# Token halves across the borders of dense stages in a two-layer streaming encoder kernel

## The reference

```
x += 0.5 * post(SwiGLU_1(pre(x)))
h  = pre(x); P = h @ w_in            # attention, recurrence and convolution inputs
x += post(concat(A, B, C) @ w_out)
x += 0.5 * post(SwiGLU_2(pre(x)))

def rms_norm(x, g):
    return x * rsqrt(mean(x * x, axis=-1) + EPS) * g
```

## Time and profile before

| | |
|---|---|
| time, median of 3 runs (lowest to highest) | 3127.04 us (3125.63 to 3131.36) |
| the profiled execution's own time | 3130.29 us |
| its span | 3128.5 us |
| PE busy | 2851.9 us, 91% |
| DVE busy | 1490.7 us, 48% |
| ACT busy | 943.2 us, 30% |
| POOL busy | 476.5 us, 15% |
| mean granted TensorE clock | 0.944 of full |
| PE idle before the lead's products, on DVE's low part (L390) | 55.1 us over 28 waits |
| DMA share of 16 engines' span, main queue | 19.5% |

### The profile page before, as it was taken

The page is one execution under the profiler, slowest core; times in us unless marked ns, Lnnn a source line. Parts: engine busy times, 40 slices in busy tenths (PEclk is TensorE's granted clock), DMA queues, the critical chain, the costliest instruction groups (busy, mean ns, idle before and its releaser), DMA issues. The chain is left out here.

```text
span 3128.5 us, 43457 instructions
## 1 busy us (share of the span) xinstructions
PE 2851.9 (91%) x18052; PEld 2667.2 (85%) x18052; DVE 1490.7 (48%) x1863; ACT 943.2 (30%) x1240; POOL 476.5 (15%) x325
## 2 busy tenths in 40 slices
PE   8999997996778899999989999979957787999997
PEld 7999997895546799999989999968945477999997
DVE  5333336477764453333363324365776635442333
ACT  4221223245134233122332212233452333321222
POOL 2000002047230300000120000120671313000001
PEclk9999998998789899999999999989976898999998
DMA  4222212112011021221212121222121011212111
GB/s 153 71 71 85 69 59 77 63 68 65 16 61 54 28 95 61 74 81 65 83 54 77 61 91 62 72 71 81 35 65 76 1 68 39 84 57 91 67 61 67
DMA packets 51694, 209.59 MB, mean 67 GB/s; under 512 B 14048, under 2 KB 14432, under 8 KB 35712
## 3 DMA queue, kind: packets, MB, share of 16 engines
q1 hardware_dynamic: 50544, 205.36, 19.5%
q10 hardware_dynamic: 1040, 2.69, 0.2%
HBM read 197.85 MB, written 10.19 MB: 66 GB/s over the span
## 5 line engine op out<-in xcount | busy, mean ns | idle before, releaser
L274 PE MATMUL ps<-hr,wr 128*128 128x320 f32 x11424 | 1728.0, 313 | 90.8 <-DVE hr L390 55.1
L274 PEld LDWEIGHTS ps<-hr,wr 128*128 128x128 f32 x11424 | 1698.5, 190 | 113.2 <-issue 55.2
L274 PE MATMUL ps<-hid,wr 128*128 128x320 f32 x4224 | 620.8, 309 | 0.0
L274 PEld LDWEIGHTS ps<-hid,wr 128*128 128x128 f32 x4224 | 619.9, 188 | 0.0
L269 DVE TENSOR_TENSOR wr<-stage,wr 128x2048 fp32r<-128x2048 f32 x164 | 377.2, 2300 | 221.9 <-ACT wr L265 221.9
L265 ACT ACTIVATE wr<-stage 128x2048 fp32r<-128x2048 f32 x164 | 312.2, 1903 | 340.7 <-DVE arena L579 267.2
L562 DVE TENSOR_TENSOR arena<-ps,arena 128x640 f32<-128x640 f32 x88 | 72.5, 824 | 546.7 <-PE ps L274 545.1
L536 POOL TENSOR_TENSOR arena<-arena 128x640 f32<-128x640 f32 x28 | 44.3, 1583 | 1736.9 <-ACT arena L514 1736.9
L505 ACT ACTIVATE arena<-arena 128x640 f32<-128x640 f32 x88 | 65.1, 740 | 803.0 <-DVE arena L562 803.0
L728 POOL TENSOR_TENSOR proj<-proj,arena 128x640 f32<-128x640 f32 x120 | 206.5, 1721 | 102.7 <-ACT arena L720 88.8
L1183 PE MATMUL ps<-proj 128*128 128x256 f32 x264 | 87.4, 505 | 69.8 <-issue 44.8
(11 more groups left out here) (208 smaller groups left out, 2191.3 us busy)
## 6 DMA issues: line engine op xcount, KB each, us to landing
stage<-in_wgu SPq DMA_DIRECT2D x88, 1024.0 KB, 4.8
stage<-in_wd SPq DMA_DIRECT2D x32, 768.0 KB, 4.2
stage<-in_w_in SPq DMA_DIRECT2D x24, 1024.0 KB, 4.9
stage<-in_wd SPq DMA_DIRECT2D x32, 640.0 KB, 3.9
stage<-in_w_out SPq DMA_DIRECT2D x8, 1024.0 KB, 5.2
arena<-in_ic SPq DMA_DIRECT2D x16, 256.0 KB, 2.7
hf<-bias_table SPq DMA_DIRECT2D x2, 2048.0 KB, 10.4
arena<-in_kc SPq DMA_DIRECT2D x16, 256.0 KB, 5.9
```

The costliest lines, as they stand in the source:

```text
L274: mm = pe.matmul(out, w(s), v(t), start=start and n == 0, stop=stop and n == 2)
```

## The change

A border is passed by the tokens in two halves of 320, and the stages from the output projection of one layer to the projection of the next stand in one program block.

- The last tile before a border computes half 0 in full, then half 1. Between the products of half 1 PE sums half 0's squares and broadcasts its factor. DVE evicts the two halves apart. The last square (`direct=1`), or the last two after an output projection (`direct=2`), go from ACT to PE without POOL. In a feed-forward stage ACT now makes the next weights' high part ahead of the square of the last tile but one.
- The lead makes y, x, high, low and square in pieces of 320 columns: all channel blocks of half 0, then all of half 1. The factor is copied by ACT from PSUM to `rs` in SBUF, from where DVE reads it. Half 1's eviction, square, root and factor stand between the pieces of half 0, and so does the split of the second weight tile. POOL adds seven times for a half, without clearing `ssum`.
- PE takes two weight tiles for each channel block, and fills all eight banks: tile 0 for blocks 0 to 3 of half 0, tile 1 for the same, both for the rest; at the end blocks 6 and 7 of half 1, tile 0 first and then tile 1.
- The sums over channels of `x` squared go to columns 320 to 479 of banks in use; the sums for `y` and the factor go to banks 1 and 3.
- In the projection the first four column blocks fill eight banks. `weigh_in` moves to block 4, the logits follow in groups of three from the end of block 4 to the middle of block 8, the streams follow half a block later than before.
- `par` is loaded after the second FFN's last weights. The result is stored in 16 pieces.

The core of the diff:

```diff
+            def pe_total(self, pe, a, row, last=False):
+                src = ssum if row is None else sqb[:, row]
                 for t in range(5):
+                    mm = pe.matmul(ps[0:64, 1, 5 * a + t:5 * a + t + 1],
+                                   src[:, a * HALF + 64 * t:a * HALF + 64 * t + 64], ones[:, 0:1],
+                                   start=row is None and t == 0, stop=last and t == 4, skip_group_check=True)
...
+            def pe_products(self, pe, tile_done):
+                self.tile_done = tile_done
+                self.pe_wait_weights(pe, 0)
+                for k in range(4):
+                    pe.wait_ge(self.split, self.of_k(0, k))
+                    self.pe_part(pe, 0, k, 0)
+                    if k == 2:
+                        self.pe_middle(pe, 1)
+                self.pe_wait_weights(pe, 1)
+                for k in range(4):
+                    self.pe_part(pe, 1, k, 0)
+                self.pe_factor(pe, 1)
+                for k in range(4, KD):
+                    pe.wait_ge(self.split, self.of_k(0, k))
+                    for j in range(2):
+                        self.pe_part(pe, j, k, 0)
+                self.pe_wait_copied(pe)
+                for k in range(KD - 2):
+                    pe.wait_ge(self.split, self.of_k(1, k))
+                    for j in range(2):
+                        self.pe_part(pe, j, k, 1)
+                    if k == 1:
+                        self.pe_x_total(pe, 0)
+                    if k == KD - 3:
+                        self.pe_x_total(pe, 1)
+                pe.wait_ge(self.split, self.of_k(1, KD - 1))
+                for j in range(2):
+                    for k in range(KD - 2, KD):
+                        self.pe_part(pe, j, k, 1)
...
             def act_part(self, act):
+                self.act_y(act)
                 for k in range(KD):
+                    self.act_x(act, 0, k)
+                    if k == 1:
+                        self.act_y_square(act, 1)
+                        split_hi(act, 0, 1, self.n0)
+                    if k == 3:
+                        self.act_y_root(act, 1)
+                    if k == 5:
+                        self.act_y_copy(act, 1)
+                for k in range(KD):
+                    self.act_x(act, 1, k)
+                    if k == 2:
+                        self.act_root(act, 0)
+                self.act_root(act, 1)
...
+            def dve_y(self, dve, a, k):
+                dve.scalar_tensor_tensor(out=y[:, k, half(a)], in0=y[:, k, half(a)],
+                                         scalar=par[:, self.post + k:self.post + k + 1], in1=rs[:, half(a)], op0=ALU.mult,
...
+            def dve_part(self, dve, evict):
+                dve.wait_ge(par_in, 16 * (self.m // 3) + 16)
+                evict(0)
+                self.dve_y_rsqrt(dve, 0)
+                for a in range(2):
+                    dve.wait_ge(self.y_copied, self.of_y(a))
+                    self.dve_y(dve, a, 0)
+                    for s in range(KD + 1):
+                        if s < KD:
+                            self.dve_x(dve, a, s)
+                        if s < KD - 1:
+                            self.dve_y(dve, a, s + 1)
+                        if s >= 1:
+                            self.dve_split(dve, a, s - 1)
+                        if a == 0 and s == 2:
+                            evict(1)
+                        if a == 0 and s == 3:
+                            split_lo(dve, 0, 1, self.n0)
+                        if a == 0 and s == 5:
+                            self.dve_y_rsqrt(dve, 1)
+                for a in range(2):
+                    self.dve_rsqrt(dve, a)
...
+                down_tile(KD // 2 - 1, 0)
...
+                last_part(0, range(KB_F)).then_inc(last_half, 1)
+                pe.wait_ge(y_summed, S + KD + 1)
+                pe.wait_ge(evac, dn + KD + 1)
+                nxt.pe_total(pe, 0, None)
+                last_part(1, range(3))
+                nxt.pe_total_direct(pe, 0)
+                last_part(1, range(3, 5))
+                nxt.pe_factor(pe, 0)
+                last_part(1, range(5, KB_F)).then_inc(used, 1)
...
+                if ahead:
+                    act.wait_ge(used, dn + KD - 1)
+                    split_hi(act, KD // 2 - 1, 0, dn + 2)
+                act.wait_ge(evac, dn + KD + 1)
+                act.wait_ge(y_summed, S + KD - 1)
+                act.activation(sqb[:, 0], y[:, KD - 2], ACT.Square).then_inc(y_squared, 1)
...
+                last_part(0, range(KD)).then_inc(last_half, 1)
+                pe.wait_ge(summed, KD - 1)
+                pe.wait_ge(evac, OUTP + 5)
+                nxt.pe_total(pe, 0, None)
+                last_part(1, range(2))
+                nxt.pe_total_direct(pe, 0)
+                last_part(1, range(2, 3))
+                nxt.pe_factor(pe, 0)
+                last_part(1, range(3, KD)).then_inc(used, 1)
...
+        def BANK_OF(q):
+            return 2 * q if q < 4 else 2 * (q % 2)
+        SELECT_FROM, LOGIT_STEPS, TAPS_FROM, TAPS_EACH = 4, 8, 11, 3
...
+                def beside(q, second):
+                    u = 2 * (q - SELECT_FROM) + second
+                    if u == 0:
+                        weigh_in()
+                    elif u < LOGIT_STEPS + 1:
+                        for n in LOGITS_AT[u - 1]:
+                            logit(n)
...
+                lead.pe_products(pe, block_done)
+                for q in range(4, NB):
+                    n, c, _ = BLOCKS[q]
+                    if c == 0:
+                        pe.wait_ge(w_lo, PROJ + n + 1)
+                    pe.wait_ge(p_evac, {4: 1, 5: 2}.get(q, q - 1))
```

More of the change, by code:

```diff
@@ L15 @@
+from collections import namedtuple
 from contextlib import ExitStack
@@ L294, in pair_of_tiles, with half, __init__ @@
             mm.then_inc(used, 1)
[L296 to L301, removed]
+        def half(a):
+            return slice(a * HALF, (a + 1) * HALF)
         class Lead:
-            def __init__(self, m, n0, factor, post, pre):
+            def __init__(self, m, n0, factor, post, pre, direct=1):
@@ L328, in pe_start, with pe_middle, pe_x_total @@
                 mm.then_inc(self.y_factor, 1)
[L330 to L336, removed]
+            def pe_middle(self, pe, a):
+                self.pe_total(pe, a, None)
+                self.pe_total_direct(pe, a)
+            def pe_x_total(self, pe, a):
+                pe.wait_ge(self.summed, self.sums(a) + KD - 1)
+                for c in range(2):
+                    mm = pe.matmul(ps[:, 4 * a + 2 * c, HALF:HALF + 160], ones[:], ssum[:, half(a)][:, 160 * c:160 * c + 160],
+                                   start=True, stop=True)
+                mm.then_inc(self.total, 1)
@@ new lines, in pe_part, with pe_wait_weights @@
+            def pe_part(self, pe, j, k, a):
+                for c in range(2):
+                    at_ = k * 256 + 128 * c
+                    mm = three(pe, ps[:, 4 * j + 2 * c + a, 0:HALF], lambda s: wr[:, j, s, at_:at_ + 128],
+                               lambda t: hr[:, t, k, half(a)], k == 0, k == KD - 1)
+                    if a and k == KD - 1:
+                        self.tile_done(mm, j, c)
+            def pe_wait_weights(self, pe, j):
+                pe.wait_ge(w_lo, self.n0 + j + 1)
+                pe.wait_ge(evac, self.n0 + j + 1)
@@ new lines, in dve_rsqrt @@
+            def dve_rsqrt(self, dve, a):
+                dve.wait_ge(self.root, 2 * self.m + a + 1)
+                dve.reciprocal(rs[:, half(a)], rs[:, half(a)]).then_inc(self.rsqrt, 1)
+            def dve_part(self, dve, evict):
[18 more added lines that the diff above has]
+                            self.dve_y_rsqrt(dve, 1)
+                for a in range(2):
+                    self.dve_rsqrt(dve, a)
+                dve.wait_ge(self.rsqrt, 2 * self.m + 2)
@@ new lines, in evict_last @@
+            def evict_last(dve, a):
+                if a:
+                    dve.wait_ge(used, chunks[1][3] + KD)
+                else:
+                    dve.wait_ge(last_half, f + 1)
+                dve.tensor_tensor(y[:, KD - 1, half(a)], y[:, KD - 1, half(a)], ps[:, 4 + a, 0:HALF],
+                                  ALU.add).then_inc(nxt.y_evicted, 1)
+                if a:
+                    dve.sem_inc(evac, 1)
+            return Stage(sync, tensor, scalar, gpsimd, vector), evict_last
@@ new lines, in evict_last @@
+            def evict_last(dve, a):
+                if a:
+                    dve.wait_ge(used, OUTP + 4)
+                else:
+                    dve.wait_ge(last_half, 1)
+                for c in range(2):
+                    cp = dve.tensor_copy(y[:, KD - 2 + c, half(a)], ps[:, 4 + 2 * c + a, 0:HALF])
+                cp.then_inc(nxt.y_evicted, 1)
+                if a:
+                    dve.sem_inc(evac, 1)
+            return Stage(sync, tensor, scalar, gpsimd, vector), evict_last
@@ L789, in build, with project_and_select @@
```

(2 more changed lines are left out.)

1143 lines of the change are left out of this document (598 added, 545 removed).

## The result

The changed kernel takes 3148.66 us (median of 4 runs, 3145.86 to 3150.56), the kernel before 3128.53 us beside it. The ratio on record is 1.0058, with an interval of 1.0046 to 1.0070 (the two medians alone would give 1.0064): slower, by 0.58%. The forecast had 3129. The time lies inside the wide range (3100 to 3150), at its edge, and outside the likeliest case's own (3118 to 3140).

A forecast was written before the change was run, and what follows sets the result against it. The prediction took PE, busy 91% of the span, plus its holes as the bound. Gains of 6.1, 3.9 and 1.7 us less losses of 2.8 and 11.1 gave -2.2: 3127.0 + 2.2 = 3129 us, range 3100 to 3150.

The forecast's parts named there:

- the likeliest case: Whole kernel: the sum as worked out, 3129 us, with its own range of 3118 to 3140; chance 0.48.
- The opening: Kernel start: tile 2 in effect at 72.9 us against 61.8, where there was no hole; 11.1 us lost.
- The holes behind the two tiles: Before tile 2: nothing covers eviction to weights, so PE stands 7.1 us after an FFN; in the projection tile 2 starts at 59.25.
- POOL's add held by the weight split: Last tile before an FFN border: DVE's low part holds up POOL's add, so PE waits 1.4 us.
- The clock's term for the sparse work: Lead, 13.85 to 20.6 us: a second clock fall slows block 2, sums and block 3; 2.5 us, bounds 0 and 3.5.
- Half 0: Lead behind an FFN: DVE begins half 0's y at 12.2 us and half 1 at 32.75.
- Half 1: Lead behind an FFN: DVE starts at 32.75 us, last low part at 48.4, POOL's last add at 49.3.
- Block 4's logits: Projection: the first logits wait behind block 4 for `wi_t` and `wall`, a new stall of 2.1 us.
- the end: Kernel's end: 21.8 us against 23.5, so 1.7 us gained.
- The overlap wins: Rival: no clock fall in the sparse stretch, POOL's add not held, broadcasts cost 1.1; 3110, down to 3100 us; chance 0.24.
- DVE and POOL pace half 1: Rival: POOL's adds hold all three DVE operations, 0.9 us each, 2.7 at each of five borders; 3142 us; chance 0.24.
- The holes are covered: Rival: evictions start earlier, leaving only 4 us of hole in each of five places; 3114 us; chance 0.04.

The follow-up runs named there:

- e3: Changed kernel with tile 2's weights split before Silu and hidden values, or the projection's first key copies; 3131.42 us, ratio 1.0003 to the kernel before.
- e4: Changed kernel with ACT's square before the weight split in a feed-forward stage's last tile but one; 3142.54 us, ratio 1.0039 to the kernel before.
- e5: Changed kernel with the root of half 0's sum behind channel block 5 in place of block 2; 3137.61 us, ratio 1.0028 to the kernel before.
- e10: e6 plus the opening's tile 1 after tile 0, with POOL's adds cut to 40 columns from each half's second; 3094.11 us, ratio 0.9893.
- e6: Changed kernel with the edits of e3, e4 and e5 together; 3108.03 us, ratio 0.9929 to the kernel before.
- e9: e6 plus the opening's tile 1 after tile 0, and half 1 evicted one step earlier; 3092.09 us, ratio 0.9890 to the kernel before.
- e8: Changed kernel with POOL's adds cut to 40 of 320 columns from each half's second add on; 3129.51 us, ratio 1.0004 to the kernel before.

## Why the prediction was right and where it was wrong

- *The opening, right in mechanism, and closer than its terms.* 11.1 us lost were forecast, 11.2 measured. Tile 2 starts at 71.34 where 69.65 stood (the 102 matmuls from 35.63 take 16.76 us where 15.0 is full speed), with 1.7 us of clock in place of 3.2: two misses that cancel by luck. The hole itself is 7.16 us.
- *The holes behind the two tiles, right.* 7.1 us were forecast in the FFN stages and 5.6 in the projection (59.25 less 53.6); 7.99, 7.16 and 6.50 are there, ended by the weights' low part. From the last low part to tile 2: 12.35 and 10.85 forecast, 12.0 and 10.5 measured. e3 shows the cause: moving the two weight parts ahead of Silu and the hidden values takes 17 us back.
- *POOL's add held by the weight split, right in size* (1.4 forecast, 1.33 measured), *wrong in what it brings.* The forecast let the clock fall only in the sparse stretch behind the tile. It fell in the last tile, to half for 10 us, and the second sums, the broadcast and the fifteen matmuls took 1.7 to 1.9 times as long as at full clock. DVE's first y came at 14.3, 13.6 and 13.4 us after E, not 12.2. e4 shows it: without the pause the clock holds there. The clock's term for the sparse work was 2.5 us with a bound of 3.5; at the first border some 3.9 us went to it, 2.1 up to the first y and 1.8 in the 30 matmuls of the next point.
- *Half 0 mis-sized.* From its first y to half 1's first the forecast had 20.55 us; 23.6 to 24.5 were measured behind the FFNs. The 30 matmuls before the second broadcast took 6.2 to 7.2 us at a low clock, where 4.4 stood, and DVE's weight part 2.97 where 2.3 did: only y, x and the low part had been given a price for the add beside them, not this.
- *Half 1, a step left out.* The forecast had 15.65 us (32.75 to 48.4); 17.67 were measured, and 15.8 in e5. Block by block the price was right. What failed is the order of ACT's work: the forecast has no term for `act_root(0)`, which stands behind block 2's high part and closes a circle of waits through PE's sum. The price is 1.86 us of half 1 at each of five places; over the five leads e5 takes 6.6 us back, and 9.4 by its time. The diff shows the root there; the forecast counted a root only behind half 1.
- *Block 4's logits and the end, nearly right:* 2.1 forecast and 2.42 measured; 21.8 and 20.6.
- *The rivals.* "The overlap wins" did not happen: the clock fell. One of the forecast's signs of being wrong came: the last low part was to be within 3 us of 36 us after the first y, and comes at 41.2. "DVE and POOL pace half 1" has its mark too (the last add after 49.3 us from E; it ends at 55.2), and its time of 3142 is nearer than 3129. Its price is not the cause: it asked 0.9 us for an add, and 0.63 was measured (e10), close to the forecast's 0.6. What made half 0 and half 1 longer are the low clock and the root. "The holes are covered" is refuted.
- *The mean of the executions.* The spans' difference misses the forecast's by 13.3 us. The other 6 of the 20 lie in the executions profiled: before, it was 3.3 us above the median that the forecast started from (3127.0), after, 2.8 us below.
- *The range.* The sum missed by 20 us and lies 8.7 us outside its own range. That 3148.66 is inside 3100 to 3150 is owed to the room left for the rival at 3142, whose price for an add did not come true: luck, by 1.3 us.

Nothing here says that halves are wrong for this border. With three orders mended the changed kernel is 22 us faster than the kernel before (e6), with all five edits 34 (e9). Whether e3's order, the weights first, would also help the kernel before was not tried.

## What to carry to other kernels

When a change makes two pieces of work end together, list what each engine does next and put first what the bound engine waits for: here two weight parts ahead of Silu were worth 17 us. For each instruction inserted into another engine's stream, ask who makes its input and what that one is waiting for; a root placed three blocks early made half 1 1.9 us longer at each of five leads. A pause of about a microsecond in front of sparse matmuls is to be priced with the clock behind it, not by its length.

## What the runs showed of the hardware

- The granted clock fell to half behind a pause of only 1.33 us, when small sums and a broadcast followed it, and held with the same sums and broadcast where the pause was absent (in e4, and at the end of the changed kernel itself: broadcast 2.39 us against 1.32). It stayed at half for 10 us while PE was never idle (508.20 to 518.30).
- Moving DVE's factor from PSUM to SBUF made y subject to POOL's adds: 0.55 us alone, 1.17 beside an add, where the PSUM form had kept 0.87 at twice the width. The Trainium skill, "SBUF — State Buffer", section "Who interferes with whom", has a DVE instruction with two SBUF inputs contend with a GpSimd one that reads SBUF; this trace agrees for y, x, the low part, and the weights' low part (2.97 us in place of 2.29). What an add of 128x320 (1.06 us in the mean) costs DVE is less than the add: 0.52 us over all leads (e8), 0.63 in half 1 (e10).
